# Key scores of the decode samples on TensorE, in a four-layer hybrid trunk step

## The reference

```python
k_past = cache_k[ic][page_table].reshape(Bs, past, N_HEADS, 2, QK_DIM)
v_past = cache_v[ic][page_table].reshape(Bs, past, N_HEADS, HEAD_DIM)
k_all = jnp.concatenate([k_past, kn], axis=1)
v_all = jnp.concatenate([v_past, vn], axis=1)
...
s = jnp.einsum('bqhcd,bkhcd->bhcqk', q, k) * (QK_DIM ** -0.5)
s = s - alibi_slopes()[None, :, None, None, None] * dist
p = jax.nn.softmax(s, axis=-1)
a = p[:, :, 0] - lam * p[:, :, 1]
return jnp.einsum('bhqk,bkhd->bqhd', a, v)
```

## Time and profile before

| | us |
|---|---|
| median of 3 runs | 2290.24 |
| lowest and highest run | 2288.85, 2290.85 |
| the profiled execution | 2291.34 |
| its span, first to last instruction | 2289.1 |
| PE busy in the span | 2109.4 (92%) |
| DVE busy | 1119.6 (49%) |
| ACT busy | 945.2 (41%) |
| POOL busy | 346.2 (15%) |

### The profile page before, as it was taken

One profiled execution on the slowest core, in us unless ns is written; L12 is line 12 of the kernel. 1 busy time (PEld: TensorE's weight loads), 2 busy tenths in 40 slices (PEclk: granted clock), 3 DMA queues, 4 the chain that ended last, 5 costly groups with the idle time before them and its releaser, 6 DMA issues. The chain is left out here.

```text
span 2289.1 us, 40799 instructions
## 1 busy us (share of the span) xinstructions
PE 2109.4 (92%) x16620; PEld 2034.7 (89%) x16620; DVE 1119.6 (49%) x1449; ACT 945.2 (41%) x1261; POOL 346.2 (15%) x291
## 2 busy tenths in 40 slices
PE   2899999999889999999999747999999939999998
PEld 1899999999379999999999646999999939999998
DVE  5644443359955444433566774544442274444321
ACT  3434432255754343322677513434332234344221
POOL 4200000148911000010111351100001040000000
PEclk9999999999899999999999868999999969999999
DMA  4233333242013333332632342333333222333331
GB/s 136 71 92 90 88 87 91 85 110 74 19 33 92 92 92 92 87 92 78 172 115 79 107 120 58 90 92 92 92 87 92 69 56 83 92 91 89 89 104 51
DMA packets 345051, 201.46 MB, mean 88 GB/s; under 512 B 7465, under 2 KB 337481, under 8 KB 344932
## 3 DMA queue, kind: packets, MB, share of 16 engines
q1 hardware_dynamic: 341460, 193.20, 29.3%
q0 software_dynamic: 3504, 7.06, 1.1%
HBM read 193.50 MB, written 8.60 MB: 88 GB/s over the span
## 5 line engine op out<-in xcount | busy, mean ns | idle before, releaser
L867 ACT ACTIVATE w_hi<-raw 128x1024 fp32r<-128x1024 f32 (+1 forms) x332 | 344.6, 1038 | 1002.7 <-PE acc L481 1001.1
L481 PE MATMUL acc<-xin_hi,w_hi 128*128 128x260 f32 x3456 | 702.7, 284 | 4.1 <-DVE w_lo L1194 3.8
L481 PE MATMUL acc<-xin_hi,w_lo 128*128 128x260 f32 x3456 | 697.5, 284 | 0.0
L481 PE MATMUL acc<-xin_lo,w_hi 128*128 128x260 f32 x3456 | 696.4, 283 | 0.0
L1194 DVE TENSOR_TENSOR w_lo<-raw,w_hi 128x1024 fp32r<-128x1024 f32 (+1 forms) x332 | 403.5, 1216 | 343.0 <-ACT w_hi L867 342.9
L481 PEld LDWEIGHTS acc<-xin_hi,w_hi 128*128 128x128 f32 x3456 | 534.6, 189 | 15.7 <-issue 11.2
L481 PEld LDWEIGHTS acc<-xin_hi,w_lo 128*128 128x128 f32 x3456 | 534.0, 189 | 0.0
L481 PEld LDWEIGHTS acc<-xin_lo,w_hi 128*128 128x128 f32 x3456 | 533.0, 189 | 0.0
L481 PE MATMUL acc<-h_hi,w_hi 128*128 128x260 f32 x1408 | 284.7, 283 | 0.0
L481 PE MATMUL acc<-h_hi,w_lo 128*128 128x260 f32 x1408 | 283.0, 282 | 0.0
L481 PE MATMUL acc<-h_lo,w_hi 128*128 128x260 f32 x1408 | 283.0, 282 | 0.0
(11 more groups left out here) (274 smaller groups left out, 1970.8 us busy)
## 6 DMA issues: line engine op xcount, KB each, us to landing
raw<-in_ffn_w_gate SPq DMA_DIRECT2D x88, 512.0 KB, 3.9
raw<-in_ffn_w_up SPq DMA_DIRECT2D x88, 512.0 KB, 3.8
raw<-in_ffn_w_down SPq DMA_DIRECT2D x64, 512.0 KB, 3.9
raw<-in_ffn_w_down SPq DMA_DIRECT2D x32, 384.0 KB, 3.5
raw<-in_attn_w_qkv SPq DMA_DIRECT2D x24, 512.0 KB, 4.0
raw<-in_conv_w_in SPq DMA_DIRECT2D x16, 512.0 KB, 4.0
raw<-in_conv_w_out SPq DMA_DIRECT2D x8, 512.0 KB, 3.9
in_mix<-in_cache_k SPq DMA_DIRECT2D x8, 512.0 KB, 3.8
```

What stands on the lines that cost most here:

```text
L481: last = pe.matmul(acc[:, b + h, 0:HALF], w[:, w_tile * P:(w_tile + 1) * P], v[:, h * HALF:(h + 1) * HALF], start=start and t == 0, stop=s ...
L867: act.activation(w_hi[n.slot(2)][:, 0:cols], raw[:, n.slot(4), 0:cols], ACT.Copy).then_inc(split_hi, 1)
```

## The change

The samples' scores are made by PE from turned key pages.

- `turn_keys(n0, n1)` on PE turns the key pages in place: 32 banks (`KEY_BANKS`) of four 128 x 128 transposes, through banks 0 to 2 of `acc`. `take_keys` copies them back over the page, two of three banks on ACT and the third on DVE. They are spread over steps h = 8 and 9 in threes, with the last eight behind.
- The queries go to `q_cols`: for a sample and a head 16 columns, zero but for two, which hold one half's 64 channels each. POOL writes them a head at a time (two copies in place of one, so `saved_s` counts four a head), after a memset before the QKV stage. `spread_query`, `take_query`, `key_product` and `key_scores` go, and with them POOL's key products.
- `score_keys(t)` multiplies: for t (samples 0 to 3, then 4 to 7) 8 heads x 4 samples, 256 columns each, summed over the heads into bank 3 of `acc`, each sample in its own 32-column group. A row is now a sample, a head and a half, and the two t lie side by side. `score_new_keys` does the same with the new keys, 64 products of one column.
- A row's softmax ends with its factor, `m_dec` (the half's sign and lambda from `half_sign`). Instead of subtracting rows and turning them, PE multiplies the exponentials with a selection matrix `select` (each row's factor at its head's column), which turns them and takes the difference in one product. ACT copies that to `a_cols`, and the new token's weight to `a_new`.
- `turn_back` uses three banks, and the heads from 3 on are turned between the groups of value products; value page 3 now joins at the same place in the first group.
- SP: value pages 1, 2, 6 and 7 wait for the first `score_keys` and stand behind pages 3 to 5, and so behind `pv_done` and `oss_done`.

```diff
-            for b in range(1, 3):
-                sp.wait_ge(s_cols_ok, b)
-                page(v_place[b], cache_v, b, vpage_in[b])
 
             sp.wait_ge(pv_done, 3 * HEADS)
             sp.wait_ge(oss_done, HEADS)
...
             for b in range(3, 6):
                 page(v_place[b], cache_v, b, vpage_in[b])
-            for b in range(6, DEC):
-                sp.wait_ge(s_cols_ok, b - 3)
+            sp.wait_ge(keys_scored, 1)
+            for b in (1, 2, 6, 7):
                 page(v_place[b], cache_v, b, vpage_in[b])
...
+                def turn_keys(n0, n1):
+
+                    for n in range(n0, n1):
+                        b, p = divmod(n, 4)
+                        if n == 0:
+                            pe.wait_ge(evacuated, TILE["w_o"])
+                        if n >= 3:
+                            pe.wait_ge(keys_dve if n % 3 == 2 else keys_act, key_takes(n - 3))
+                        if p == 0:
+                            pe.wait_ge(kpage_in[b], 32)
+                        for j in range(2):
+                            for e in range(2):
+                                last = pe.transpose(acc[:, n % 3, (2 * j + e) * P:(2 * j + e + 1) * P],
+                                                    k_place[b][:, j, (2 * p + e) * P:(2 * p + e + 1) * P], ident)
+                        last.then_inc(keys_turned, 1)
+
+                def score_keys(t):
+                    last_bank = KEY_BANKS // 2 * (t + 1) - 1
+                    pe.wait_ge(keys_act, max(key_takes(n) for n in range(last_bank + 1) if n % 3 < 2))
+                    pe.wait_ge(keys_dve, max(key_takes(n) for n in range(last_bank + 1) if n % 3 == 2))
                     for h in range(HEADS):
-                        r = sample_row(b, h)
-                        last = pe.matmul(acc[:, 2 * (b % 2) + h // 4, (h % 4) * P:(h % 4 + 1) * P],
-                                         qs[:, r:r + 1].to_broadcast([P, P]), ident, start=True, stop=True)
-                    last.then_inc(q_all_ready, 1)
+                        for g in range(4):
+                            last = pe.matmul(acc[32 * g:32 * g + 2 * HEADS, 3, t * PAST:(t + 1) * PAST].rearrange("p (j c) -> p j c", j=2),
+                                             q_cols[:, t, g, h, :], k_place[4 * t + g][:, :, h * P:(h + 1) * P],
+                                             start=h == 0, stop=h == HEADS - 1)
+                    last.then_inc(keys_scored, 1)
...
-                for b in range(POOL_PAGES, DEC):
-                    spread_query(b)
+                pe.wait_ge(saved_s, 4 * HEADS)
+                turn_keys(24, 27)
+                score_keys(0)
+                turn_keys(27, KEY_BANKS)
                 pe.wait_ge(o_taken, HEADS)
                 for j, src in enumerate((ks, vs)):
                     last = pe.transpose(bank7[:, j * P:(j + 1) * P], src[:], ident)
                 last.then_inc(rows_s_full, 1)
-
-                pe.wait_ge(k_prod_dve, DEC - POOL_PAGES)
-                for h in range(4):
+                score_new_keys()
+                score_keys(1)
+                for h in range(3):
                     turn_back(h)
...
+                def take_keys(i):
+                    for n in range(3 * i, min(3 * i + 2, KEY_BANKS)):
+                        act.wait_ge(keys_turned, n + 1)
+                        b, p = divmod(n, 4)
+                        act.activation(k_place[b][:, :, 2 * p * P:2 * (p + 1) * P], acc[:, n % 3, :].rearrange("p (j c) -> p j c", j=2),
+                                       ACT.Copy).then_inc(keys_act, 1)
...
-                    page = k_place[b]
-                    q = q_flat[b % 2][:].unsqueeze(1).to_broadcast([P, 2, D])
-                    pool_e.tensor_tensor(page[:], page[:], q, ALU.mult).then_inc(k_prod_pool, 1)
+                pool_e.memset(select[:], 0.0).then_inc(dec_zeroed, 1)
```

More of the change, by code:

```diff
@@ L138, in constants @@
         for h in range(HEADS):
-            c[sample_row(b, h), C_POS:C_POS + PAST] = 2.0 ** -(h + 1.0) * (np.arange(PAST) - PAST) / SCALE
             c[sample_row(b, h), C_MASK + h] = 1.0
+    for g in range(4):
+        for h in range(HEADS):
+            for half in range(2):
+                row = 32 * g + 2 * h + half
+                c[row, C_POS:C_POS + PAST] = 2.0 ** -(h + 1.0) * (np.arange(PAST) - PAST) / SCALE
+                c[row, C_SEL + HEADS * g + h] = 1.0
+                c[row, C_HALF + half] = 1.0
     for g, win in enumerate(WINDOWS):
@@ L347, in trunk_step @@
         vpage_in = [sem(f"vpage_in{s}") for s in range(DEC)]
[L348 to L352, removed]
+        keys_turned, keys_act, keys_dve, keys_scored, dec_zeroed, factors_ok, weighted = (
+            sem(n) for n in ("keys_turned", "keys_act", "keys_dve", "keys_scored", "dec_zeroed", "factors_ok", "weighted"))
+        s_rows_full, dec_max_ok, dec_exp_ok, select_ok, a_dec_full, a_cols_ok = (
+            sem(n) for n in ("s_rows_full", "dec_max_ok", "dec_exp_ok", "select_ok", "a_dec_full", "a_cols_ok"))
         rows_s_full, rows_s_taken, os_in_ok, os_sq_ok, os_scaled, os_back = (
@@ new lines, in score_new_keys @@
+                def score_new_keys():
+                    pe.wait_ge(s_taken, 3 * HEADS)
+                    for t in range(2):
+                        for h in range(HEADS):
+                            for g in range(4):
+                                r = sample_row(4 * t + g, h)
+                                last = pe.matmul(pair[32 * g:32 * g + 2 * HEADS, 1, t:t + 1], q_cols[:, t, g, h, :], ks[:, r:r + 1],
+                                                 start=h == 0, stop=h == HEADS - 1)
+                    last.then_inc(s_rows_full, 1)
@@ L818, in attention @@
                                 g = b % 4
-                                last = pe.matmul(pair[32 * g:32 * g + 32, t, :], a_cols[:, j, b, :],
+                                last = pe.matmul(pair[32 * g:32 * g + 32, t, :], a_cols[:, b // 4, j, g, :],
                                                  v_place[b][:, j, t * 512:(t + 1) * 512],
@@ L1073, in take_head @@
                     if h == 0:
-                        act.wait_ge(s_cols_ok, DEC)
-                    act.activation(mix_hi[:, h, 0:SEQ], acc[:, h % 4, :], ACT.Copy, scale=sub_gain[:]).then_inc(mix_hi_ok, 1)
+                        act.wait_ge(keys_scored, 2)
+                    act.activation(mix_hi[:, h, 0:SEQ], acc[:, h % 3, :], ACT.Copy, scale=sub_gain[:]).then_inc(mix_hi_ok, 1)
                 for h in range(HEADS + 2):
@@ L1137, in attention @@
                 act.wait_ge(a_dec_full, 1)
-                for t in range(2):
-                    act.activation(spread[:, :, t, :, HEADS * t:HEADS * t + HEADS], turned[:, :, :, t, :], ACT.Copy)\
-                       .then_inc(a_cols_ok, 1)
+                act.activation(a_cols[:].rearrange("p t j g m -> p (t j g m)"), bank6[:], ACT.Copy).then_inc(a_cols_ok, 1)
+                act.activation(a_new[:], bank7[:, 0:1], ACT.Copy).then_inc(a_cols_ok, 1)
                 for h in range(2, HEADS):
@@ L1650, in _ @@
             step(dve.tensor_scalar(sub_gain[:], vec[:, V_SUB:V_SUB + 1], 1.0 - LAMBDA_INIT, None, ALU.mult))
+            dve.wait_ge(ident_in, 16)
+            step(dve.scalar_tensor_tensor(half_sign[:], const[:, C_HALF + 1:C_HALF + 2], neg_lam[:], const[:, C_HALF:C_HALF + 1],
+                                          ALU.mult, ALU.add))
             pool(0)
@@ L1758, in save @@
                     pool_e.tensor_copy(to[:, h, 0:2, :], src[:, SEQ:T].rearrange("p (u g) -> p u g", u=2)).then_inc(saved_s, 1)
+                pool_e.wait_ge(stored, 16 * STORED["conv"])
+                step(pool_e.memset(q_cols[:], 0.0))
                 pool_e.wait_ge(units_done, UNIT["qkv"])
@@ L1769, in _ @@
                         pool_e.wait_ge(qkn_ready, 2 * h + 2)
-                        save(qs, h, qn)
+                        for c in range(2):
+                            here = slice(c * QK, (c + 1) * QK)
+                            pool_e.tensor_copy(q_cols[here, :, :, h, 2 * h + c], qn[here, SEQ:T].rearrange("p (t g) -> p t g", t=2))\
+                                  .then_inc(saved_s, 1)
+                            pool_e.wait_ge(saved_s, 4 * h + 2 + c)
                         save(ks, h, kn)
```

198 lines of the change are left out of this document (96 added, 102 removed).

## The result

The changed kernel took **2274.74 us** (median of 4 runs, 2271.91 to 2276.16), the kernel before beside it 2289.55 us (4 runs, 2288.37 to 2290.85). The ratio is 0.9934, 95% interval 0.9919 to 0.995: faster by 14.8 us. The direction was right; the gain is 5.7 us larger than forecast, and rival 1 (full clock throughout, 2276 us) is what happened.

What follows compares the result with a forecast made beforehand. Bound: the attention drain (1289.7 to 1400.54 us), finally its value-page look-ups. T 1331.5, plus 47.5 for pages and 3.4 for last products, gives 1382.4 against 1391.5; 9.1 us off 2290.24 forecasts 2281.1 us, range 2276 to 2289.

Steps and rivals of the forecast that it cites:

- rival 1: Full clock throughout, because added banks close PE's gaps: T = 1326.3, 14.3 us less, 2276 us; chance 0.18.
- Leg one: First stretch of the attention drain, from the last QKV products (1289.7) to T; DVE holds others up there.
- part 2: Key-bank work entering leg one: T = 1326.3 at full clock, 1338.3 at half, 1331.5 mixed (clock 0.79).
- T: When the last head's sums of squares (o_ss) are written, ending leg one; 1342.4 us before, forecast 1331.5.
- five terms (5.5 us): DVE copies 1.3, late-bank wait 1.0, banks before score piece and weights 0.9, before values 1.3, ACT's copies 1.0.
- part 1: What leaves leg one: three DVE steps unblocked (15.0 us), reductions 2.2 and 4.4; T = 1320.8 with nothing put in.
- part 3: Value pages bind: 14 half-page look-ups behind T, 3.17 us apart, landed T + 47.5; products end 1382.4, 9.1 us less.
- Leg two: Second stretch of the drain, from T to 1378.6 before: the samples' scores and softmax.
- part 4: Leg two's new score work stays hidden: turned weights (a_cols) at 1366.0, just before value page 2 lands at 1366.3.
- Rival 3: Slower through one-column products: if weight loads show in full, 26.8 us more, 2306 to 2307; chance 0.08 (with rival 4).
- The 9.0 us behind the value products: Stretch from the last value products (1391.5) to the output projection (1400.54); forecast to stay as it is.
- The rule against it: The Trainium skill says transposes don't count as PE busy or engage full clock; set aside because the trace disagrees.

## Why the prediction was right or wrong

**The failed step is the clock in part 2.** Leg one's walk at full clock gave T = 1326.3; the trace has 1325.7. I had then mixed in 43% of a half-clock walk, from the mean clock of before (0.74), for 5.2 us more (0.43 x 12.0), and that was nearly the whole miss. The end of the value products came out 6.1 us below the forecast (1376.35 against 1382.4): -5.8 from T, -0.5 from the pages (T + 47.0, not 47.5), +0.2 from the last group. The measured clock of leg one was 1.00, not 0.79: with GpSimd's products gone it rises from 0.74 to 0.86, and with the transposes to between 0.95 and 1.00. My own sum had removed the one and put in the other; the mean should have gone with them. A second error may lie beneath: I priced the half clock at 12.0 us, as if PE would then bound T. Where the clock did fall for some 4 us, with all the transposes there, T was 1324.5 to 1326.1, and 1324.7 to 1325.7 where it held. Half clock throughout leg one was seen only with a quarter of the transposes, so the 12.0 themselves are untested. The full-clock walk's 1326.3 is close, but whether its five terms (5.5 us) are right one by one or only in their sum, no run shows.

**What leaves leg one (part 1)** was right, step by step and nearly in its sizes: 0.75, 0.17 and 0.75 us, where I had 0.6, 0.17 and 0.75. Both experiments on GpSimd's products confirm the cause.

**The value pages (part 3)** were right: 14 half pages, 3.16 us apart (forecast 3.17), PE's last wait is for the last page. In T + 47.0 smaller errors cancel: the first issue came at T + 1.9, not 2.7, and the last landing took 4.0 us, not 3.6. The four halves more behind T were a loss that the change brought in, and taking only their look-ups away gave 8.6 us; I had them in the sum but didn't draw that out.

**Leg two (part 4)** was hidden, as forecast, but on wrong sizes. I had a_cols at 1366.0, "just fits"; it was there at 1345.3. Of these 20.7 us, 7.5 are the first score product's, which ended at 1327.3 and not 1334.8 (the clock term again, 0.43 x 16.2 = 7.0), 14.2 the one-column products' (15.4 taken, 1.20 measured: eight-column transposes were the wrong neighbour), and 2.2 the banks and the second score product; 3.3 go the other way. The softmax was taken too short: 6.5 us from the scores (1335.24) to the selection product (1341.74), not 4.2, because GpSimd's scaling of the heads now runs beside it. With the one-column products five times over the scaling was done before, and the same steps took 3.75 us (1351.91 to 1355.66); of the 2.75 less, 1.6 are the two steps of DVE that write `select`, here in the changed kernel and then in that run:

```profile
1339.70 1.99 DVE L1626 TENSOR_SCALAR select<-const,m_dec 128x32 f32<-128x32 f32 x2
```

```profile
1355.22 0.39 DVE L1626 TENSOR_SCALAR select<-const,m_dec 128x32 f32<-128x32 f32 x2
```

Nothing of that reached the end. Rival 3 is refuted: the price at which it decides, 0.14 us a product, is 15 times the measured one.

**The 9.0 us behind the value products** stayed 9.0 (1376.35 to 1385.35). The projection's first products ran at the half clock for a shorter time, to 1389.0, 3.6 us against 5.7 before; that is about the 1.2 us between 15.2 and the spans' 16.4.

**The rule against it** on transposes was rightly set aside; the run with a quarter of them turned that from an argument into a measurement (0.67 over leg one, against 0.95 to 1.00).

## What to carry to other kernels

A mean clock, or any other mean of a stretch, comes out of the waits and the work in it: when a change removes the waits, don't carry the old mean over. Work out what PE does in the new stretch, and ask first whether T hangs on PE's clock at all. When two engines' long steps always coincide, shrink one of them in the kernel before: one run tells what the contention is worth, and what it would leave unchanged. And before moving transfers behind a bound, count the scalar look-ups in front of them: fourteen of 3.16 us were worth 13.7 and 17.3 us here (2274.74 less the two medians), with not one byte less moved.

## What was unexpected of the hardware

- PE stopped for its own instructions: 2.7 us in the middle of 256-column products with 400 GB/s on the DMA engines, and up to 5.0 us after each 128 passes of one column. One packet of instructions holds 256. Short passes are cheap to compute (9.5 ns) and dear to bring in: 21.8 us for 512 of them, 43 ns each, where nothing hid it.
- 128 passes of one column with weights of 16 columns, in four column groups of 32, took 1.20 us at the full clock, though a single product with full 128-column weights had two weight loads of 0.33 us before, at half clock.
- DVE steps that read a single big tile are held up by GpSimd as well: t_buf (a scaling of 128 columns, twice) lasted 2.26 us beside its products, and 0.55 in the changed kernel (from 1303.13 us). Steps that read the scores from PSUM were not: two of 512 columns took 0.68 and 0.69 us beside a key product in the kernel before (from 1323.57 and 1324.18 us), and 0.69 each with GpSimd idle in the changed kernel (from 1314.63 and 1315.25).
